# Decay attention by running products of gates in place, instead of logarithms, running sums and exponentials

## What is computed

```python
q = silu(q_raw); v = i_raw
f = lb_dir + (1 - lb_dir) * sigmoid(f_raw)        # one gate per token and channel, for each direction
k, logf = 1 - f, log(f)
# per direction and head (gla_chunk_scan), b = cumsum(logf):
scores[t, s] = sum_d q[t, d] * exp(b[t, d] - b[s, d]) * k[s, d]      # s <= t; the other direction on flipped tokens
o[t] = sum_s scores[t, s] * v[s]
o = rms_norm(o_forward + o_backward, norm_g) * silu(g)
```

## Time and profile before

| | us |
|---|---|
| median of 3 runs | 2708.49 |
| lowest and highest | 2698.99, 2708.79 |
| the profiled execution's own time | 2709.19 |
| its span | 2707.4 |

### The profile page before, as it was taken

One profiled execution on the slowest core, in us unless ns is written; L12 is line 12 of the kernel. 1 busy time (PEld: TensorE's weight loads), 2 busy tenths in 40 slices (PEclk: granted clock), 3 DMA queues, 4 the chain that ended last, 5 costly groups with the idle time before them and its releaser, 6 DMA issues.

```text
span 2707.4 us, 41182 instructions
## 1 busy us (share of the span) xinstructions
PE 2494.2 (92%) x16196; PEld 2015.4 (74%) x16196; DVE 1825.1 (67%) x1932; ACT 1189.0 (44%) x1050; POOL 103.7 (4%) x154
## 2 busy tenths in 40 slices
PE   5879999976798999999999985699999999999998
PEld 2358888833686888888888862388788888888886
DVE  6976666678756776776767659767766666544445
ACT  4643333355535333334443455733453333444444
POOL 1020000000001000000000011000020000000000
PEclk9989999977799999999999987799999999999999
DMA  9997888722453888887888848678657777555551
GB/s 285 409 337 256 285 277 280 260 70 87 156 177 110 284 282 277 283 286 277 291 285 295 284 165 196 257 242 283 239 196 237 236 239 237 187 190 197 188 199 63
DMA packets 228976, 635.19 MB, mean 235 GB/s; under 512 B 33186, under 2 KB 34852, under 8 KB 208132
## 3 DMA queue, kind: packets, MB, share of 16 engines
q1 hardware_dynamic: 216164, 579.27, 63.4%
q0 software_dynamic: 9536, 34.48, 3.9%
q10 hardware_dynamic: 3168, 19.92, 1.8%
HBM read 613.83 MB, written 19.79 MB: 234 GB/s over the span
## 4 chain that ended last, share of the span: by engine, by line
PE 79%; DVE 15%; ACT 2%; issue 2%; DMA 1%; SPq 0%; DVEq 0%; ACTq 0%
PE PS L293 32%; PE PS L325 26%; PE PS L297 16%; DVE raw L1640 2%; DVE Pb L2088 2%; DVE acc L2083 2%; DVE X L1707 1%; DVE raw L1644 1%; PE PS L1082 1%; DMA araw<-in_ada_w 1%; ACT Pb L1159 1%; PE PS L1057 1%; DVE WF L1644 1%; PE PS L495 0%; DVE wlo L288 0%
## 5 line engine op out<-in xcount | busy, mean ns | idle before, releaser
L288 DVE TENSOR_TENSOR wlo<-raw,whi 128x2048 fp32r<-128x2048 f32 x368 | 844.1, 2294 | 700.4 <-ACT whi L284 699.6
L284 ACT ACTIVATE whi<-raw 128x2048 fp32r<-128x2048 f32 x368 | 705.7, 1918 | 1210.0 <-PE PS L293 786.3
L293 PE MATMUL PS<-H,whi 128*128 128x512 f32 x3840 | 1216.9, 396 | 19.1 <-DVE wlo L288 11.0
L297 PEld LDWEIGHTS PS<-H,wlo 128*128 128x128 f32 x3840 | 723.4, 188 | 165.0
L297 PE MATMUL PS<-H,wlo 128*128 128x256 f32 x3840 | 766.6, 278 | 0.0
L325 PE MATMUL PS<-whi,H 128*128 128x512 f32 x2048 | 633.6, 390 | 0.5 <-DVE H L1755 0.5
L293 PEld LDWEIGHTS PS<-H,whi 128*128 128x128 f32 x3840 | 591.8, 189 | 28.5 <-issue 21.7
L325 PEld LDWEIGHTS PS<-whi,H 128*128 128x128 f32 x2048 | 384.4, 188 | 82.3 <-issue 2.0
L325 PE MATMUL PS<-wlo,H 128*128 128x512 f32 x1024 | 398.4, 389 | 0.0
L185 DVE SCALAR_TENSOR_TENSOR acc<-araw,cact,acc 128x1024 f32<-128x1024 f32 x240 | 307.3, 1280 | 3.8 <-DMA araw<-in_ada_w 3.3
L325 PEld LDWEIGHTS PS<-wlo,H 128*128 128x128 f32 x1024 | 192.2, 188 | 39.6
(11 more groups left out here) (314 smaller groups left out, 1517.6 us busy)
## 6 DMA issues: line engine op xcount, KB each, us to landing
raw<-in_mlp_w SPq DMA_DIRECT2D x256, 1024.0 KB, 6.0
araw<-in_ada_w SPq DMA_DIRECT2D x274, 512.0 KB, 4.6
raw<-in_mix_w_in SPq DMA_DIRECT2D x64, 1024.0 KB, 7.7
raw<-in_s_w_glu SPq DMA_DIRECT2D x32, 1024.0 KB, 7.5
acc<-in_ada_w SPq DMA_DIRECT2D x40, 512.0 KB, 9.3
raw<-in_ada_w POOLq DMA_DIRECT2D x32, 512.0 KB, 4.1
raw<-in_mix_w_out SPq DMA_DIRECT2D x16, 1024.0 KB, 5.1
vmat<-Pb ACTq DMA_DIRECT2D x8, 1024.0 KB, 7.9
```

What stands on the lines that cost most here:

```text
L284: nc.scalar.activation(whi[:, s % 2, :], raw[:, s, :], ACT.Copy).then_inc(S("hi_done"), 1)
L288: nc.vector.tensor_tensor(wlo[:, s % 2, :], raw[:, s, :], whi[:, s % 2, :].bitcast(F), ALU.subtract).then_inc(S("lo_done"), 1)
L293: return nc.tensor.matmul(PS[:, b, :], w, H2[:, :, k, :], start=first, stop=last, skip_group_check=True)
L297: return nc.tensor.matmul(PS[:, b, 0:T], w, H2[:, 0, k, :], start=False, stop=last, skip_group_check=True)
```

## The change

Keys and queries are kept in place, one array of left-to-right and one of the other direction for each, so four arrays, and go from a level to the next by one multiplication with the product of gates over the neighbouring block. Those block products come from six pairwise multiplications (`longer_decays`). Each instruction of a level is cut into two halves of the heads. ACT takes no logarithms and no exponentials; for levels 0 to 4 it copies the keys of both directions into one array (`keys_together`), while PE reads the queries straight from the two arrays (`level_part`). The level-0 products and those of a token with itself move to the two sides of the normalisation's spreading. Both sets of idle products go, three gate parts move from the levels to rounds 9 and 12 of attention, and weight slabs 2 and 3 of the output projection are loaded as soon as the rotation is done.

```diff
-    GATE_SPLIT = (16, 18, 21, 24, 27, 30, 32, 32)
+    GATE_EXTRA = {9: 2, 12: 1}
+    GATE_SPLIT = (19, 19, 21, 23, 25, 27, 29, 32)
+    LV_BANK = (4, 5, 1, 2, 3, 0)
...
+    def sides(z, base, half):
+        near_far = z[:, base:base + 2 * (2048 + half)].rearrange("p (u r) -> p u r", u=2)[:, :, 0:2048]
+        return near_far.rearrange("p u (b w) -> p u b w", w=2 * half)[:, :, :, 0:half]
...
+    def level_part(z, base, half, side, o, n):
+        if 2 * half <= n:
+            at = o // (2 * half)
+            return sides(z, base, half)[:, :, at:at + n // (2 * half)].rearrange("p u b q -> p b u q")
+        return z[:, base + 2048 * side + o:base + 2048 * side + o + n]
...
     def rms_pe(pe):
+        pe.wait_ge(S("lv_x"), 1)
...
-        idle_products(8, 7)
+        for half in range(2):
+            pe.wait_ge(S("lv_key"), half + 1)
+            near(pe, 0, half, LV_BANK[0])
...
+        same_place(pe, 7)
...
+            sp.wait_ge(S("rot_done"), 4)
+            slab_loads(sp, 0, s.B, s.G, s.src, slabs=range(2, 4))
             sp.wait_ge(S("gate_used"), 32)
             slab_loads(sp, 0, s.B, s.G, s.src, slabs=range(2))
-            sp.wait_ge(S("lv_arg"), 14)
-            slab_loads(sp, 0, s.B, s.G, s.src, slabs=range(2, 4))
...
-                    if n == 9:
-                        idle_products(14, 7)
...
-                    gate_part(pe, n)
+                    for _ in range(1 + GATE_EXTRA.get(n, 0)):
+                        gate_part(pe, gates)
+                        gates += 1
...
+                for lv in range(1, 8):
+                    gates = range(GATE_SPLIT[lv], GATE_SPLIT[lv + 1]) if lv < 7 else range(0)
+                    for half in range(2):
+                        pe.wait_ge(S("lv_x"), 2 * lv + half)
+                        if lv < 5:
+                            pe.wait_ge(S("lv_key"), 2 * lv + half + 1)
...
+                        for c in gates[:1] if half == 0 else gates[1:]:
                             gate_part(pe, c)
...
-                    if n == 8:
-                        act.wait_ge(S("hg_f"), 2)
-                        for d in range(2):
-                            run(FD[d], FD[d], ACT.Ln, "hg_ln")
-                        for d in range(2):
-                            run(LN_KEY[d], (FF_, FB_)[d], ACT.Ln, "hg_ln", bias=TINY)
...
-                for lv in range(8):
-                    for w in range(2):
-                        if (lv, w) == (0, 0):
-                            continue
-                        act.wait_ge(S("lv_arg"), 2 * lv + w)
-                        run(XY[lv % 3][w], XY[lv % 3][w], ACT.Exp, "lv_exp")
...
+                for lv in range(1, 5):
+                    for half in range(2):
+                        keys_together(lv, half)
...
-                elif n < 14:
-                    log_sums((0, 3, 6, 9, 13)[n - 9], (3, 6, 9, 13, 16)[n - 9])
+                elif n < 14:
+                    decayed_query((n - 10) // 2, n % 2)
                 elif n == 14:
-                    gated(GH, SIGG, 1)
-                    v.wait_ge(S("hg_ln"), 4)
-                    link(tt(LN_KEY[0], LC[0], LN_KEY[0], ALU.subtract))
+                    link(tt(SAME, FF_, FB_, ALU.add))
+                    v.sem_inc(S("lv_x"), 1)
...
+            def longer_decays(j):
+                pair = decays(j).rearrange("p d (n u) -> p d n u", u=2)
+                link(tt(decays(j + 1), pair[:, :, :, 0], pair[:, :, :, 1], ALU.mult))
+
+            def level_up(lv):
+                w, n = 2 ** (lv - 1), 2048 >> lv
+                shape = [P, 2, n // 2, w]
+                parts = [slice(n // 2 * half, n // 2 * half + n // 2) for half in range(2)]
+                for half, blocks_ in enumerate(parts):
+                    if lv < 6:
+                        v.wait_ge(S("lv_key"), 2 * lv + half - 1)
+                    else:
+                        v.wait_ge(S("lv_mm"), level_done(lv - 1, half))
+                    keys = sides(PF, 8192, w)[:, :, blocks_]
+                    tt(keys, keys, key_ratios(lv - 1)[:, :, blocks_].unsqueeze(3).broadcast_to(shape), ALU.mult
+                       ).then_inc(S("lv_k"), 1)
+                for half, blocks_ in enumerate(parts):
+                    v.wait_ge(S("lv_mm"), level_done(lv - 1, half))
+                    queries = sides(WF, 0, w)[:, :, blocks_]
+                    tt(queries, queries, query_ratios(lv - 1)[:, :, blocks_].unsqueeze(3).broadcast_to(shape),
+                       ALU.mult).then_inc(S("lv_x"), 1)
...
-            level_arg(0)
-            level_arg(1)
+            v.wait_ge(S("vt_evac"), 8)
+            for j in range(6):
+                longer_decays(j)
             v.wait_ge(S("rms_std"), 1)
             link(nc.vector.reciprocal(RS, RS))
             v.sem_inc(S("rms_inv"), 1)
+            level_up(1)
             v.wait_ge(S("rms_wide"), 1)
             link(stt(OA, OA, SUBG, bank(0, 4), ALU.mult, ALU.mult))
             v.sem_inc(S("oa_final"), 1)
+            level_put(level_done(0), LV_BANK[0], 0)
+            level_put(3, 7, 14)
+            for lv in range(2, 8):
+                level_up(lv)
                 if lv == 5:
                     ada_finish(v, link, SCALE1, 7)
-                level_mul(lv)
...
+                if lv < 6:
+                    level_put(level_done(lv - 1), LV_BANK[lv - 1], lv - 1)
```

More of the change, by code:

```diff
@@ L420, in trunk @@
     VH = PF[:, 4096:6144].rearrange("p (h a e) -> p h a e", h=8, a=2)
-    LC = [WF[:, 0:2048], PF[:, 12288:14336]]
-    SIGQ, SIGG = WF[:, 2048:4096], WF[:, 4096:6144]
-    FD = [WF[:, 6144:8192], WF[:, 2048:4096]]
+    ARAWF = araw[:].rearrange("p a c -> p (a c)")
+    SIGQ, SIGG = WF[:, 2048:4096], ARAWF
+    FD = [WF[:, 4096:6144], WF[:, 6144:8192]]
+    QD = [WF[:, 0:2048], WF[:, 2048:4096]]
+    DECAY = [(WF, 4096), (PF, 12288)] + [(ARAWF, 2048 - 4096 // 2 ** (j - 1)) for j in range(2, 7)]
@@ new lines, in near @@
+    def near(pe, lv, half, b):
+        other = 1 if lv == 5 else 0
+        for z in range(8 * half, 8 * half + 8):
+            for q in range(4):
+                r = q ^ other
+                at = P * z + 32 * q
+                keys = KC[lv % 2][:, at:at + 32] if lv < 5 else level_part(PF, 8192, 32, q % 2, at, 32)
+                queries = level_part(WF, 0, 2 ** lv, r % 2, P * z + 32 * r, 32)
+                last = nc.tensor.matmul(PS[32 * q:32 * q + 32, b, 32 * z:32 * z + 32], keys, queries,
+                                        start=True, stop=True)
+        last.then_inc(S("lv_mm"), 1)
@@ L431, in trunk, with same_place, level_done @@
+    def same_place(pe, b):
+        for z in range(16):
+            for q in range(4):
+                at = slice(P * z + 32 * q, P * z + 32 * q + 32)
+                last = nc.tensor.matmul(PS[32 * q:32 * q + 32, b, 32 * z:32 * z + 32], SAME[:, at], QH[:, at],
+                                        start=True, stop=True)
+        last.then_inc(S("lv_mm"), 1)
+    def level_done(lv, half=1):
+        return 2 * lv + half + (2 if lv else 1)
     mx, nm, sm, rc = ([small[:, 32 + 4 * k + 2 * p:34 + 4 * k + 2 * p] for p in range(2)] for k in range(4))
@@ L936, in attention_pe @@
                     scores(n)
+                gates = 0
                 pe.wait_ge(S("rot_done"), 4)
@@ new lines, in hgrn_pe @@
+                for lv in range(1, 8):
[4 more added lines that the diff above has]
+                            pe.wait_ge(S("lv_key"), 2 * lv + half + 1)
+                        if lv == 2 and half == 0:
+                            pe.wait_ge(S("oa_final"), 1)
+                        if lv < 6:
+                            near(pe, lv, half, LV_BANK[lv])
+                        elif lv == 6:
+                            for z in range(8 * half, 8 * half + 8):
+                                for q in range(2):
+                                    last = nc.tensor.matmul(
+                                        PS[64 * q:64 * q + 64, 4 + z // 8, 64 * (z % 8):64 * (z % 8) + 64],
+                                        level_part(PF, 8192, 64, q, P * z + 64 * q, 64),
+                                        level_part(WF, 0, 64, 1 - q, P * z + 64 - 64 * q, 64), start=True, stop=True)
+                            last.then_inc(S("lv_mm"), 1)
+                        else:
+                            if half == 0:
+                                pe.wait_ge(S("sc_ready"), 2)
+                            for t in range(2):
+                                for h in range(4 * half, 4 * half + 4):
+                                    z = 8 * t + h
+                                    last = nc.tensor.matmul(PS[:, z // 4, (z % 4) * P:(z % 4 + 1) * P],
+                                                            level_part(PF, 8192, P, t, T * h + P * t, P),
+                                                            level_part(WF, 0, P, 1 - t, T * h + P - P * t, P),
+                                                            start=True, stop=True)
```

(13 more changed lines are left out.)

117 lines of the change are left out of this document (41 added, 76 removed).

## The result

The changed kernel takes 2669.15 us (median of 5 runs, 2666.79 to 2671.62) against 2707.43 before (5 runs, 2698.99 to 2708.79): a ratio of 0.9868, 95% interval 0.9852 to 0.9885, which is 35.7 us of 2707.43 (the medians lie 38.3 apart). I had forecast 2688 and a range that ended at 2673. The sign was right, the size was not: the saving is 1.7 times the 21.0 that I had worked out.

What follows compares the result with a forecast made beforehand. DVE was taken to bound the stretch from the last attention round to level 7, PE to be the longest member of attention's ring; 4.1 + 17.4 - 0.5 = 21.0 us off 2709.2 gave 2688, range 2673 to 2700.

Steps and rivals of the forecast that it cites:

- What bounds the levels: Last round of attention to level 7: DVE is the bound, busy 66.2 of 71.4 us; an instruction saved there is saved.
- Rival E: DVE's savings don't arrive because another engine was equally late; time 2705, chance 0.03.
- Rival D: In-place products with short runs are dearer, about 2.5 us each; slower than before, 2722, chance 0.03.
- Rival C: PE's strided query reads at levels 0 to 4 double the 1.94 us; 6 less saved, time 2694, chance 0.09.
- Part 1: Attention from round 9 to the squares, PE as the ring's longest member: 4.1 us saved.
- all fast: Part 1's bound at full clock: squares start at 631.5, a gain of 11.8 us.
- Rival B: PE fast, as denser work keeps the clock up: 33 us saved at most, time 2681, chance 0.14.
- Part 2: Squares to the end of level 7: 60.1 us against 77.5, 17.4 saved (13 to 21).
- the two places named: DVE's waits for PE at level 4, behind the sum after level 3, and for level 7's second key half; together 4.0.
- The clock: Idle products removed: if PE's clock falls, the normalisation's spreading takes up to twice as long, up to 2.5 us lost.
- Part 3: Behind level 7 to the output projection: 20.6 us unchanged, 0.5 lost to late weight slabs, at most 1.5.
- 20 to 22: Sign of being wrong: the stretch after level 7 isn't 20 to 22 us.

Runs made afterwards that it cites:

- keys first: Changed kernel with level 1's two key products ahead of DVE's wait for the root, before the reciprocal: 2671.07 us, 0.9868.
- without added parts: Changed kernel without the three added gate parts in rounds 9 and 12, which the levels take instead: 2672.88 us, 0.9889.
- all parts in attention: Changed kernel with all 32 gate parts in attention, two a round, none in the levels: 2670.09 us, 0.9879.
- scan experiment: Changed kernel with one more DVE scan of 0.69 us, into an unused array, in each of rounds 9 to 13: 2674.14 us, 0.9884.
- late slabs: Changed kernel with weight slabs 2 and 3 requested behind 0 and 1 and after level 6's last query product: 2669.73 us, 0.9882.
- attention part alone: Kernel before with only the attention part of the change, levels working on stale values: 2689.89 us, ratio to before 0.9952.
- products that wait: Changed kernel with each of the 28 DVE products in the levels waiting for itself: 2674.83 us, 0.9889.
- parts behind the second half: Changed kernel with all gate parts of a level behind its second half: 2667.39 us, 0.9860.

## Why the prediction was wrong, step by step

**What bounds the levels: right for the kernel before.** DVE it was: with fewer DVE instructions the stretch from the squares to the end of level 7 shrank by 21.6 us, and 0.23 us more on each of the 28 products came back as 6.9. In the changed kernel PE is nearly as late, by the runs with keys first and without added parts. Rival E (another engine equally late) falls. Rival D (dear products) falls by 1.22 us each.

Rival C, PE's strided reads, falls in its size, but not as a mechanism. The reader should compare only at one clock, for that of PE changed inside this stretch: the level-0 products (L470 at 635.51 and 635.93, queries element by element from two arrays) ran at 1.00, those of a token with itself (L479, neighbours) at 0.50.

```profile
635.51 0.28 PE L470 MATMUL PS<-WF,HF 128*32 128x32 f32 x6
...
635.93 1.54 PE L470 MATMUL PS<-WF,HF 128*32 128x32 f32 x122
638.55 3.99 PE L580 MATMUL PS<-acc,ident 12*128 12x256 f32 x16 [1.07 <-DVEq L1999]
642.47 1.94 PE L479 MATMUL PS<-Pb,HF 128*32 128x32 f32 x128
...
664.33 0.76 PE L470 MATMUL PS<-WF,HF 128*32 128x32 f32 x64
```

The last line is half of level 4, runs of 16 elements, at 1.00. The records overlap; one takes 0.196 us there and 0.213 at level 0, so the starts lie (0.76 - 0.20)/63 = 9 ns apart there and (1.54 - 0.21)/121 = 11 at level 0. Runs of two elements cost nothing: level 1's second half at 1.00, in the profile with all parts in attention, has 61 records, (0.73 - 0.20)/60 = 9 ns.

```profile
642.88 0.73 PE L470 MATMUL PS<-WF,HF 128*32 128x32 f32 x61 [1.33 <-issue]
```

So the price is 2 ns a record and 0.3 us in all, where C had 1.94 us more per level, and it lies in the shade of the normalisation. The penalty that the Trainium skill, "Advanced Engine Details and Errata", section "SBUF Cachelines", names for another line with each access agrees with this: level 0 pays, level 1 with two hits on a line doesn't.

**Part 1 failed, at its first step: "without them four rounds cost 18.5 us", 4.6 each.** I took the mean of rounds 0 to 9 and called PE the ring's longest member. That mean holds rounds with 1.76 us of gates on DVE, and rounds in which DVE waited 1.4 to 1.7 us for PE's scores. Rounds 9 to 12 after hold 1.23 us and take DVE's train, 3.72; the added parts I charged with 4.2 cost 0.45, as neighbours run side by side and most of their time passes while DVE is at work. From mix 9 to mix 13 it was 15.3 us, not 22.7: the term "18.5" should have been 14.9, and that of the parts 0.45. Even the bound that I gave as all fast, a gain of 11.8 in this part, was passed by the 12.1 measured. The trace of before had what was needed: a heavy round there, from the mix at 634.15 with a 1.23 product and a 2.29 subtraction to the next at 639.16, has no wait in it:

```profile
634.15 0.17 DVE L1853 RECIPROCAL small<-small 128x2 f32<-128x2 f32 x1
...
635.57 1.23 DVE L1862 TENSOR_TENSOR Pb<-Pb,WF 128x1024 f32<-128x1024 f32 x1
636.83 2.29 DVE L1907 TENSOR_TENSOR raw<-WF,raw 128x2048 f32<-128x2048 f32 x1
639.16 0.17 DVE L1853 RECIPROCAL small<-small 128x2 f32<-128x2 f32 x1
```

From the mix of round 11 (619.48) on, DVE's longest wait for PE was 0.19 us; in round 9 it had waited 2.66 for ACT's logarithms and in round 10 another 2.87 for PE's scores behind them. So rounds 11 to 15 were DVE's already, and what I should have done is subtract on DVE. The scan experiment shows the rule, 0.72 for 0.72. The clock of 0.70 that I carried over belongs to PE, which no round of this stretch waited for. Why it stays near 1.00 here in the light rounds, and between 0.70 and 0.90 in rounds 0 to 9 of otherwise equal code, is not settled. From mix 13 to the squares it was 11.0 against my 11.6, and whether PE or DVE sets that last stretch no run tells apart.

Rival B (PE fast, at most 33 us saved) came nearest in number. Its clock came true in attention, 1.00, but not in the levels, 0.82, and the scan experiment shows that with PE at 1.00 a round still takes DVE's train.

**Part 2, sizes.** Squares to the reciprocal's end: 8.5 forecast, 10.5 in this profile, since the channel sum ran 5.9 us at a clock of 0.67; at 1.00 it took 3.4 (the run with late slabs) and the whole 8.0. Why the clock was low there is open. DVE's train: 43.2 forecast, 40.3 measured (638.44 to 681.11, less 2.3 of waits), the starts every 1.14 instead of 1.26 would be 28 x 0.12 = 3.4. Waits: 4.0 forecast, 2.3 measured, and in one of the two places named (level 7's keys); behind the sum after level 3 DVE waited for nothing. Tail to the end of level 7: 4.4 forecast, 2.8 measured. So 2.9, 1.7 and 1.6 better, 2.0 worse: 21.6 us saved for the 17.4 forecast.

**The clock**: taking the eight idle products out of the normalisation cost nothing, for putting them back costs 2.7. No run puts the fourteen of round 9 back alone.

**Part 3**: no loss by the slabs, and 18.3 us from level 7 to the output projection where I had left the former length, 19.9 by the first product (740.72): PE's clock was 0.91 there in place of 0.81. Outside 20 to 22 was one of my own signs of being wrong. That this follows the change is not shown: the kernel before with the attention part alone had 18.3 too, and two of the changed kernel's variants (products that wait, parts behind the second half) had 0.81 and 19.9 again.

**Chances.** Faster by over 0.5% had 0.83 and came. The range ended 4 us above the median. Of the 35.3 us in the two large lines, 21.0 were forecast; of the 14.3 beyond, 8.0 are part 1, where PE was taken for the limit, 4.2 part 2 and 2.1 part 3, of which 1.6 isn't shown to be the change's.

## What to carry to other kernels

Where engines work in a ring, find the bound for each kind of round by whether its train has a gap, not from a mean over rounds with different work; then subtract or add on that engine. Before pricing an instruction, look whether its neighbour uses other strips of the array, and whether it will still wait for itself. Halving instructions pays where two engines hand one array back and forth: here 10.9 us of 74.6. Before two durations on PE are compared, see that both ran at one clock.

## What the runs showed of the hardware that I had not expected

- Products with 128x32 weights in different strip pairs run beside each other: 1.05 us for one gate part, 1.06 for two, 1.91 for three.
- A VectorE instruction of 1.22 us starts every 1.14 us when it only signals, 1.26 (before, 643.33 to 644.59) when it waits for itself, and 1.37 when a separate signal follows the wait.
- Reading a moving operand element by element from two arrays 8 KB apart cost TensorE 11 ns a record against 9 at 32 columns and clock 1.00; with runs of two elements it was 9 again.
- The same channel sum of 16 records took 3.4 or 5.9 us in different executions, at a clock of 1.00 or 0.67 over the normalisation.
